# Moving the hyena filters' work from expert groups 4 to 11 to groups 7 to 14, and leaving their memory to the weight stream for longer

## The reference

```python
(silu(xb @ w_gate[e]) * (xb @ w_up[e])) @ w_down[e]      # 1024 -> 512 -> 1024
```

```python
h = jnp.sin(fr1 * (z @ w1 + b1))          # z: 256 positions x 33 features
h = jnp.sin(fr2 * (h @ w2 + b2))          # 64 wide
h = h @ w3                                # 2 x 512 taps, times a decay
Kf = jnp.fft.rfft(k, n=2 * L, axis=0)     # the filter's spectrum
```

## Time and profile before

| | us |
|---|---|
| median of 3 runs (1652.52 to 1653.62) | 1652.74 |
| the profiled execution | 1651.14 |
| its span, from the first to the last instruction | 1649.3 |
| TensorE's matmuls busy in it | 1590.3 |
| the first product of group 0 starts at | 269.67 |
| the last product of group 14 (unit 212) starts at | 689.73 |
| the first product of group 15 starts at | 701.08 |

### The profile page before, as it was taken

How to read it: one execution, slowest core, us unless ns; L and a number is a source line. 1 busy time by engine, 2 the same in 40 slices (tenths; PEclk the granted TensorE clock), 3 DMA queues, 4 the chain that set the end, 5 groups by cost and what they waited for, 6 DMA issues and landing times.

```text
span 1649.3 us, 22868 instructions
## 1 busy us (share of the span) xinstructions
PE 1590.3 (96%) x9309; PEld 1199.4 (73%) x9309; DVE 940.6 (57%) x1600; ACT 730.8 (44%) x1391; POOL 94.3 (6%) x83
## 2 busy tenths in 40 slices
PE   7999997999999999789999999999999999999998
PEld 6997884444334334239997889999789978889997
DVE  5967655222332332237675567766767756677665
ACT  6755542101110010036663447655666643575554
POOL 1010001000000000014001000000230010000000
PEclk9999998999999999999999999999999999999999
DMA  9434577999999999984344445555444444545550
GB/s 358 176 128 145 200 283 286 378 393 424 423 424 403 424 424 424 423 364 175 133 169 163 166 155 192 190 191 180 162 157 150 168 165 157 185 168 181 187 195 26
DMA packets 57414, 399.82 MB, mean 242 GB/s; under 512 B 6612, under 2 KB 7029, under 8 KB 9946
## 3 DMA queue, kind: packets, MB, share of 16 engines
q1 hardware_dynamic: 57306, 398.32, 62.5%
HBM read 397.24 MB, written 1.05 MB: 241 GB/s over the span
## 4 chain that ended last, share of the span: by engine, by line
PE 85%; DMA 9%; DVE 3%; ACT 1%; issue 1%; SPq 0%; DVEq 0%
PE P L171 83%; DMA RING<-in_ws_dram 7%; PE P L174 2%; DMA ez<-in_ws_dram 1%; DMA W<-in_hw_dram 1%; DVE RINGL L183 1%; DVE X L189 0%; ACT WH L177 0%; DVE SM L189 0%; DVE rl_mix L189 0%; ACT JNK L177 0%; DVE YB L183 0%; ACT L180 0%; DVE RT L189 0%; DVE HS L189 0%
## 5 line engine op out<-in xcount | busy, mean ns | idle before, releaser
L183 DVE TENSOR_TENSOR RINGL<-RING,WH 128x1024 fp32r<-128x1024 f32 x338 | 419.9, 1275 | 131.0 <-ACT WH L177 129.8
L177 ACT ACTIVATE WH<-RING 128x1024 fp32r<-128x1024 f32 x351 | 358.2, 1055 | 53.7 <-PE P L171 50.7
L171 PE MATMUL P<-HA,WH 128*128 128x256 f32 x1208 | 345.1, 286 | 0.0
L171 PE MATMUL P<-LA,WH 128*128 128x256 f32 x1208 | 340.3, 282 | 0.0
L171 PE MATMUL P<-HA,RINGL 128*128 128x256 f32 x1208 | 340.3, 282 | 0.0
L171 PEld LDWEIGHTS P<-HA,WH 128*128 128x128 f32 x1208 | 227.7, 189 | 5.8 <-issue 3.0
L171 PEld LDWEIGHTS P<-HA,RINGL 128*128 128x128 f32 x1208 | 228.3, 189 | 2.1
L171 PEld LDWEIGHTS P<-LA,WH 128*128 128x128 f32 x1208 | 228.6, 189 | 0.0
L171 PE MATMUL P<-RING,XT 128*64 128x512 f32 x632 | 143.5, 595 | 7.0 <-DMA RING<-in_ws_dram 7.0
L171 PEld LDWEIGHTS P<-RING,XT 128*64 128x64 f32 x632 | 44.2, 137 | 101.6 <-issue 79.7
L183 DVE TENSOR_TENSOR GS<-P,GS 128x512 f32<-128x512 f32 x16 | 11.1, 692 | 180.2 <-PE P L171 180.2
(11 more groups left out here) (403 smaller groups left out, 2689.8 us busy)
## 6 DMA issues: line engine op xcount, KB each, us to landing
RING<-in_ws_dram SPq DMA_DIRECT2D x288, 1024.0 KB, 5.0
ew<-in_ws_dram SPq DMA_DIRECT2D x47, 1024.0 KB, 20.8
ez<-in_ws_dram SPq DMA_DIRECT2D x16, 1024.0 KB, 19.8
ek<-in_ws_dram SPq DMA_DIRECT2D x6, 1024.0 KB, 10.4
ef<-in_ws_dram SPq DMA_DIRECT2D x4, 1024.0 KB, 10.7
eha<-in_ws_dram SPq DMA_DIRECT2D x2, 1024.0 KB, 4.8
ela<-in_ws_dram SPq DMA_DIRECT2D x2, 1024.0 KB, 6.6
TAB<-in_dft_dram SPq DMA_DIRECT2D x2, 1024.0 KB, 5.6
```

Source lines behind the costliest of these rows:

```text
L171: return self.engine.matmul(*a, **k) if self.engine else self
L177: return self.engine.activation(*a, **k) if self.engine else self
L183: return self.engine.tensor_tensor(*a) if self.engine else self
```

## The change

The filters' eight steps move three groups later: filter 0 to the groups 7 to 10, filter 1 to 11 to 14. The loads of the tables and weights move with them (behind units 105 and 165 in place of 69 and 129). The five places that the filters' tiles need take stream units up to 92 in place of 60 (TABLES_FREE), and `ek1` up to 188 in place of 104 (K1_FREE). ScalarE's wait before it copies the spectra names the last unit before these bounds. With 7 + 12 places less those that have closed, 17 are in use for the units up to 92 where 12 were for those from 61 on, and then 12 until 188 where 11 were from 105 on. For example, the load of unit 70 follows unit 53 in place of 56, that of 72 unit 55 in place of 60.

```diff
@@ -251,9 +251,10 @@
 
 
 EXTRA = ("ek1", "egs", "ez", "ef2", "ef1", "ext", "eha", "ela", "ew0", "ew1", "ew2", "ewr")
-ONCE = U_MOE + 12
-LAST_UNIT = {"egs": ONCE, "ext": ONCE, "ef1": U_MOE + 28, "ef2": U_MOE + 28, "eha": U_MOE + 28, "ela": U_MOE + 28,
-             "ewr": U_MOE + 28, "ek1": U_MOE + 6 * UNITS_PER_GROUP, "ez": U_B2, "ew0": U_B2, "ew1": U_B2, "ew2": U_B2}
+
+ONCE, TABLES_FREE, K1_FREE = U_MOE + 12, U_MOE + 5 * UNITS_PER_GROUP, U_MOE + 13 * UNITS_PER_GROUP
+LAST_UNIT = {"egs": ONCE, "ext": ONCE, "ef1": TABLES_FREE, "ef2": TABLES_FREE, "eha": TABLES_FREE, "ela": TABLES_FREE,
+             "ewr": TABLES_FREE, "ek1": K1_FREE, "ez": U_B2, "ew0": U_B2, "ew1": U_B2, "ew2": U_B2}
 FIRST_HOMES = {33: "ek1", 34: "egs", 35: "ez", 36: "ef2", 37: "ef1", 38: 5, 40: 6, 41: "eha", 42: "ela", 43: 0, 39: "ext",
                44: 1, 45: "ew0", 46: 2, 47: 3, 48: 4, 49: "ew1", 50: "ew2", 51: "ewr"}
 
@@ -2197,7 +2198,7 @@
 
 
 
-FILTER_FIRST = 4
+FILTER_FIRST = 7
 FILTER_PRODUCTS = ((0,), (8,), (16, 17, 18, 19), (22, 23, 24, 25))
 FILTER_LATE = ((0,), (8,), (16, 17, 18, 19), ())
 FILTER_EARLY = ((1, 2, 3, 4, 5, 6), (9, 10, 11, 12, 13, 14), (20, 21), ())
@@ -2244,16 +2245,16 @@
         if v in m.follow:
             e.wait_ge(*s.unit[v])
             fetch(e, m, s, A, m.follow[v])
-        if v == first_unit(3):
+        if v == first_unit(FILTER_FIRST - 1):
             sync_tables(e, m, s, A)
             sync_filter(e, m, s, A, 0)
-        if v == first_unit(8):
+        if v == first_unit(FILTER_FIRST + 4):
             sync_filter(e, m, s, A, 1)
     e.dma_start(m.GF2[:, :], A["g_final"].partition_broadcast(128)).then_inc(*s.g_final_in.up(0))
 
 
 def sync_tables(e, m, s, A):
-    e.wait_ge(*s.unit[60])
+    e.wait_ge(*s.unit[TABLES_FREE - 1])
     e.dma_start(m.TF[:, :, :, :], A["dft"][:, 0:1024]).then_inc(*s.dft_in.up(0))
     e.dma_start(m.DEC[:, :, :], A["decay"]).then_inc(*s.decay_in.up(0))
     e.dma_start(m.ZP[:, :], A["zpos"]).then_inc(*s.zpos_in.up(0))
@@ -2485,7 +2486,7 @@
     if 22 <= i < 26:
         kind, h = (i - 22) // 2, i % 2
         e.wait_ge(*s.product["filter", l, kind, h])
-        e.wait_ge(*s.unit[first_unit(7)])
+        e.wait_ge(*s.unit[(K1_FREE if l else TABLES_FREE) - 1])
         e.activation((m.K1 if l else m.K0W)[:, kind, h, :], m.P[m.bank["spectrum", l, kind, h]][:, :],
                      ACT.Copy).then_inc(*s.evac.up("filter", l, kind, h))
```

## The result

Over 20 runs each, the changed kernel takes 1654.82 us and the kernel before 1652.86; the ratio is 1.0013, 95% interval 1.0007 to 1.0019, so 2.1 us more (1.2 to 3.1). The prediction said 3.2 us more, 1655.9, and its range of 1652.5 to 1658.6 holds the measured time; the 3.2 itself lies just outside the interval of the difference. The difference is within the 0.2% that I had set as "no difference", with the sign of the forecast. The profiled execution took 1653.12 us (span 1651.3), against 1651.14 (1649.3).

What follows compares the result with a forecast made beforehand. The experts' stream of loads, 2.47 us a unit, was taken to set the end through unit 212's product. Stream lead -3.5, spectra +6.9, -0.3 and +0.1 gave +3.2 us, so 1655.9 us, range 1652.5 to 1658.6.

Steps and rivals of the forecast that it cites:

- The homes: Stream at 320 to 350 us: longer-open homes let loads issue earlier, filling 3.8 us of idle (bounds zero and 4.7).
- The tables in a full stream: Tables and filter weights sent into a full stream cost 5.1 us against 4.8 before, leaving the stream 3.5 us ahead.
- The spectra: Group 14, between products and downs: filter 1's spectra add 6.9 us on TensorE, with no stream-paced group behind.
- The wait that grows: Group 11: TensorE waits 4.7 us for filter 1's weights, caught up by group 13 with 1.5 us to spare.
- The sum: Unit 212's product, last of group 14, moves by -3.5 + 6.9 - 0.3 + 0.1 = +3.2 us.
- TensorE's side of the sum: Group 14's last product: TensorE's own work reaches it at 676.3 us, the same moment as the stream's load.
- The signs: Changed profile: no 300 to 430 us window under 400 GB/s, dip about 445, unit 212's product at 692 to 693.5.
- (b): Group 11's wait for filter weights isn't caught up by group 13; two us over gives +5.2, 1657.9; 10%.
- (c): Homes closing at units 76 to 92 leave holes, so the stream isn't ahead: +6.6 us, 1659.3; 7%.
- (d): The 5.69 us idle after group 14 swallows a later group 14, so the kernel is faster, 1649.2; 9%.
- (e): Stream gain nearer the windows' 4.7 us, tables costing no more than before: +1.9 us or less, 1654.6; 14%.
- (a): The sum for unit 212's product holds, +3.2 us; its own range is 1654.5 to 1657.3; 60%.

Runs made afterwards that it cites:

- move_only: The changed kernel with filters in groups 7 to 14 but the homes of the kernel before; 1.0033 of the kernel before, +5.5 us.
- first5_old_homes: Filters in groups 5 to 12, as in first5, but with the homes of the kernel before; 1.0001 of the kernel before, +0.2 us.
- first5: The change two groups earlier: filters in groups 5 to 12, tables' homes until unit 80; 0.9971 of the kernel before, -4.8 us.
- early_w: The changed kernel with filter 1's weights issued four units earlier, behind unit 161 in place of 165; 1.0013 of the kernel before, +2.1 us.
- spectra_twice: The changed kernel with the products of filter 1's spectra done twice in group 14; 1.0052 of the kernel before, +8.6 us.
- first6: The change one group earlier: filters in groups 6 to 13, layer 1's filter place until unit 176; 0.9988 of the kernel before, -2.0 us.
- k1_home_old: The changed kernel with layer 1's filter place leaving the stream at unit 104 in place of 188; 1.0013 of the kernel before, +2.1 us.

## Why the prediction was right, point by point

- **What bounds it.** That unit 212's product decides, and group 15 merely follows, held in every kernel: 5.44 to 5.71 us of idle after group 14, whatever came before. From group 15's start to the end of the span it is 947.3 to 949.2 us in all twelve traces, so the span moves as group 15 does. Unit 212's product itself, the fourth of the downs, starts at 686.67 + 3 x 1.72 = 691.8, where the prediction had 692.8.
- **The homes.** Right, and shown by taking them away alone in two places: 3.4 us with the filters in the groups 7 to 14 (move_only against the change), 4.9 with 5 to 12 (first5_old_homes against first5), each to some 2.4 us. I took 3.8 from the landings; the windows' 4.7, which I had as the upper bound, is as near to the measured pair.
- **The tables in a full stream.** Right in place: the dip is at 440 to 450 us, 345 GB/s. Filter 1's weights were undersized: I took 1.9 us of lost rate from the earlier trace rows, and the window in group 11 shows (424 - 300) / 424 x 10 = 2.9. Why the same bytes cost one us more there than in group 8 is open. I put the lost rate down to small transfers, and read the 344 GB/s as agreeing. The packets in the trace say that this is the lesser part. The 97 packets of 256 bytes (W1 and W2) took 0.023 us each, before and after; that is mostly overhead, as the stream's 8 KB in 0.31 us would make it 0.010, but together it is only some 0.14 us of the 16 engines. What is slow meanwhile are the large ones. While the small packets pass, the stream's packets of 8 KB take 0.52 us each in the changed kernel and 0.49 in the kernel before, against 0.31 ahead of it.
- **The spectra, 6.9 us.** Right: 686.67 - 679.72 = 6.95 in the trace, and removed or doubled they show in full in the time.
- **The wait that grows.** I said 4.7 us, caught up by group 13 with 1.5 to spare. It was 3.77: the weights let TensorE go on at 596.0, not 598.0, and TensorE came at 592.3, not 593.3. Group 13's last two products waited for their loads (0.61 us at 645.68), and taking the wait away changed nothing. By the Trainium skill (DMA: Bandwidth & Descriptors, Rules for kernel authors) a DMA is to be issued early and waited for late; early_w does so and gains nothing, because here a later wait for the stream absorbs the early one: early_w's product of group 13 waits 0.91 us for its load where the changed kernel's waits 0.61, and starts at the same distance from group 0 (376.8 and 376.7 us).
- **The sum.** +3.2 predicted, +2.1 measured (1.2 to 3.1). The two traces differ by the same three terms as predicted: the stream -4.6 at group 13, the spectra +6.95, and some -0.3 for the wait of unit 212 that went away. The mechanism is right; the term that is off is the stream's lead, 3.5 predicted and 4.6 in the traces, of which 0.7 stood already at group 0. That it came so near is in part luck, as the windows of 10 us of the two traces show. Their difference in bytes from 260 to 650 us, divided by 424 GB/s, is an estimate of the lead: 1.2 us from before 300 us, a head start that isn't the change's; 4.9 from 300 to 350, the filled holes, for which I took 3.8; -0.7 from 350 to 450, the tables; and -1.0 from 450 to 650, filter 1's weights, for which I took no difference. Together 4.4, and 3.2 without the head start. So the holes and the weights were each about one us off, in opposite directions. The runs, in which head starts average out, still say +2.1 and not +3. Where their last us comes from is open: move_only, which has the holes, also lies 1.1 us under its 6.6.
- **TensorE's side of the sum.** I had both sides meet at 676.3 for group 14's last product. They do meet, at 675.4: unit 208 lands as TensorE gets there. VectorE is done with the taps at 670.4, 9 us before they are asked for, so it costs nothing, as assumed.
- **The signs.** As said, no window from 300 to 430 us is under 400 GB/s (the lowest has 419), the dip is at 440, TensorE's first wait for a load is in group 7 (450.36), the downs of group 14 have no load in front of them and the idle isn't shorter. Not as said: the wait for W is under 4 us, unit 212 comes just before 692, and group 14's products don't run from load to load; none of them shows a wait.
- **The rivals.** (b), the filter weights' wait, is refuted by early_w. (c), that the stream isn't ahead, by the windows; what it would have cost is near move_only, +5.5 measured for +6.6. (d), the idle that swallows the delay, by spectra_twice and move_only. (e), the larger gain of the stream, had +1.9, which is nearer to the measured +2.1 than (a)'s +3.2: by the number (e), with 14%, is nearer, though (a)'s own range of 1654.5 to 1657.3 holds the measured 1654.82 as well; and its filled holes are the traces' 4.9 us. Its other half, tables that cost no more than before, is not borne out (-0.7).

## What to carry to other kernels

In a stretch that a stream of loads bounds, the computing engine's extra work is free only if enough of that stretch is left behind it to catch up: here a group of 12 units gave back some 3.7 us (in first6 the spectra's 6.95 us in group 13 are a lag of 679.13 - 646.20 - 29.65 = 3.3 us at group 14's last product), so 7 us of work wanted two groups behind it, and had none. In the last group before the bound changes hands such work costs its full length. So an edit that buys the stream time (longer homes) and one that moves work later (to make the homes possible) should be priced apart: here they are worth about -4.9 and +7, and a place two groups earlier keeps the first and pays nothing for the second that the runs show.

## What I had not expected of the hardware

- The granted clock after the 3.77 us wait: the window of 590 to 600 us has 0.74, a mixture of the two levels (2.4 GHz until late in the wait, 1.2 GHz after it: 596 to 600 us has 0.50), and the next two down units took 3.47 and 2.30 us in place of 1.72. So the wait cost another 2.3 us on its spot, and neither reached the end. Shorter waits at the same place did it too: after 2.20 us in the kernel before, 510 to 520 us has 0.83, and after 1.77 us in move_only 600 to 610 has 0.83.
- The stream's arrival differs between single executions of kernels that take the same time. k1_home_old and the change have the same ratio, but group 15 starts at 706.53 and 703.13 in their traces, and group 0 accounts for 1.7 of these 3.4 us (270.61 and 268.95). Differences of one or two us are to be taken from the runs, not from two traces.
- 0.28 MB of filter weights, in packets of 256 bytes to 4 KB, held the rate to 300 GB/s over a window in group 11 and 344 in group 8, with the DMA engines at a full share both times (1.02). It isn't the small packets' own time that is lost: the stream's 8 KB packets take some 0.5 us in place of 0.31 meanwhile. What slows them is open; W3, one transfer of 256 KB in packets of 4 KB, passes at the same time, and no run sends it alone.
